# Tokens turned before their modulation is known, and three accumulator banks for the convolution stretch

## The reference, cut to what matters

```python
shift, scale, gate = split(silu(c) @ mod_w[li] + mod_b[li], 3)       # the same for c_ctx
hx = rms_norm(x, norm_w[li]) * (1.0 + scale) + shift
hc = rms_norm(ctx, norm_w[li]) * (1.0 + scale_c) + shift_c
```

## Time and profile before

| | |
|---|---|
| median of 3 runs | 1190.12 us (1187.65 to 1192.85) |
| the profiled execution's own time | 1189.36 us |
| its span in the trace | 1187.4 us |
| PE busy | 1113.2 us, 94% |
| DVE busy | 590.1 us, 50% |
| ACT busy | 359.4 us, 30% |
| POOL busy | 182.0 us, 15% |
| mean granted PE clock | 0.984 |
| DMA | 94.16 MB, mean 79 GB/s |

### The profile page before, as it was taken

One profiled execution on the slowest core, in us unless ns is written; L12 is line 12 of the kernel. 1 busy time (PEld: TensorE's weight loads), 2 busy tenths in 40 slices (PEclk: granted clock), 3 DMA queues, 4 the chain that ended last, 5 costly groups with the idle time before them and its releaser, 6 DMA issues.

```text
span 1187.4 us, 11863 instructions
## 1 busy us (share of the span) xinstructions
PE 1113.2 (94%) x4259; PEld 595.1 (50%) x4259; DVE 590.1 (50%) x1219; ACT 359.4 (30%) x822; POOL 182.0 (15%) x174
## 2 busy tenths in 40 slices
PE   3797889999998999999999999999999999999988
PEld 0474455545554444555544444444545555556654
DVE  0335356737683746676621114530346563446776
ACT  1522021214442234455410112111324433343450
POOL 2200100027772310000000001320012120000000
PEclk9899899999998999999999999999999999999999
DMA  9722404136667011001001104220110220200001
GB/s 309 286 71 75 141 1 142 68 123 202 201 219 247 34 54 39 16 1 54 1 1 56 68 0 155 71 71 24 48 66 6 72 106 1 72 1 1 1 1 71
DMA packets 47201, 94.16 MB, mean 79 GB/s; under 512 B 2870, under 2 KB 4567, under 8 KB 47143
## 3 DMA queue, kind: packets, MB, share of 16 engines
q1 hardware_dynamic: 42693, 81.41, 19.8%
q10 hardware_dynamic: 3330, 8.67, 2.0%
q0 software_dynamic: 1120, 3.32, 1.0%
HBM read 91.17 MB, written 2.23 MB: 79 GB/s over the span
## 4 chain that ended last, share of the span: by engine, by line
PE 87%; DVE 6%; DMA 4%; issue 1%; ACT 1%; SPq 1%; POOL 0%; DVEq 0%; ACTq 0%
PE ps L715 47%; PE ps L965 10%; PE ps L893 7%; PE ps L1001 4%; PE ps L1023 3%; PE ps L865 2%; DVE pool_mem L1154 2%; PE ps L912 2%; PE ps L877 2%; PE ps L944 2%; PE ps L1013 2%; PE ps L934 2%; DMA ring<-in_mod_w_dram 2%; PE ps L732 2%; PE ps L754 1%
## 5 line engine op out<-in xcount | busy, mean ns | idle before, releaser
L715 PE MATMUL ps<-ring,hT 128*128 128x512 f32 (+1 forms) x832 | 345.6, 573 | 2.2 <-DVE hT L1138 2.2
L715 PEld LDWEIGHTS ps<-ring,hT 128*128 128x128 f32 x832 | 156.7, 191 | 172.6 <-issue 165.0
L715 PE MATMUL ps<-hT,ring 128*128 128x512 f32 (+1 forms) x512 | 174.9, 500 | 15.5 <-DVE pool_mem L1154 15.5
L715 PEld LDWEIGHTS ps<-hT,ring 128*128 128x128 f32 x512 | 99.6, 197 | 85.4 <-issue 77.8
L1767 POOL TENSOR_SCALAR stat<-stat 128x8 f32<-128x8 f32 (+3 forms) x52 | 22.8, 439 | 717.6 <-DVE stat L1326 238.4
L893 PE MATMUL ps<-ring,hT 128*128 128x512 f32 x192 | 88.9, 594 | 0.8 <-DVE pool_mem L1381 0.8
L965 PE MATMUL ps<-ring,hT 128*128 128x512 f32 x192 | 85.7, 593 | 2.1 <-DMA ring<-in_ev_w_out_dram 2.1
L1358 DVE TENSOR_REDUCE stat<-ps 128x1 f32<-128x768 f32 x64 | 60.9, 952 | 52.4 <-PE ps L1001 52.2
L1425 DVE TENSOR_TENSOR pool_mem<-ps,pool_mem 128x512 f32<-128x512 f32 x36 | 24.8, 688 | 92.7 <-PE ps L965 87.5
L1768 POOL TENSOR_TENSOR stat<-stat 128x8 f32<-128x8 f32 (+3 forms) x52 | 66.4, 1278 | 4.3
L1154 DVE SCALAR_TENSOR_TENSOR pool_mem<-ps,halftap,pool_mem 128x254 f32<-128x254 f32 (+3 forms) x96 | 59.1, 616 | 3.4
(11 more groups left out here) (198 smaller groups left out, 1392.4 us busy)
## 6 DMA issues: line engine op xcount, KB each, us to landing
ring<-in_mod_w_dram SPq DMA_DIRECT2D x11, 2048.0 KB, 8.0
ring<-in_od_w_in_dram SPq DMA_DIRECT2D x8, 2048.0 KB, 8.3
ring<-in_ev_w_in_dram SPq DMA_DIRECT2D x7, 2048.0 KB, 8.2
pool_mem<-la_rows_dram SPq DMA_DIRECT2D x24, 512.0 KB, 7.0
ring<-in_ev_w_out_dram SPq DMA_DIRECT2D x4, 1536.0 KB, 6.6
ring<-in_od_w_out_dram SPq DMA_DIRECT2D x2, 2048.0 KB, 7.7
ring<-in_mod_w_dram ACTq DMA_DIRECT2D x1, 2048.0 KB, 14.3
xs_all<-in_x_dram POOLq DMA_DIRECT2D x4, 512.0 KB, 8.9
```

The source lines that it names most:

```text
L715: mm = pe.matmul(bank[:, 0:width], lhs_of(k), rhs_of(k), start=(k == 0), stop=(k == count - 1))
```

## The change

Beginning: the six token tiles are loaded first, from ACT's queue. SP loads only the identity, `pick` and the first parameter rows, then `mod` 0 to 3 and `kvdt` at once (`mod` 3 and `kvdt` have places of their own in memory that is free then), then the second parameter rows and the other constants. POOL's eight broadcast loads come after the last `norm`. A new stage `trt` turns a normalised tile, and DVE (first four feature blocks) and ACT (last four) copy it to `hT` as it is; a new stage `hmod` scales and shifts `hT` in place, a third of the tokens at a time, each third before two `kvdt` tiles. `params` 1 moves behind `kvdt` 1, three small DVE operations into `dtv`.

Convolution stretch: from `kvdt` 0 to the last `diag`, units take the least recently used of banks 0, 1 and 7, and `diag` is a unit.

Scan: fillers are `mod` in steps 1, 3, 5, 7 and 9 and `ga` in steps 2, 4, 6, 8, 10 and 11; step 0 has none.

The diff, cut to its core:

```diff
@@ stages_layer0
-    st = [("params", 0), ("params", 1)]
-    st += [("mod", 0, 0), ("mod", 0, 1), ("modsum", 0, 0), ("mod", 0, 2), ("modsum", 0, 1)]
-    st += [("norm", 0, t) for t in range(NT)]
-    st += [("mod", 0, 3), ("modsum", 0, 2), ("modsum", 0, 3), ("modcol", 0)]
-    st += [("trn", 0, k, 0) for k in range(KD)] + [("trn", 0, k, 1) for k in range(0, KD, 2)]
+    st = [("params", 0), ("norm", 0, 0), ("norm", 0, 1), ("trt", 0), ("norm", 0, 2), ("trt", 1), ("mod", 0, 0)]
+    st += [("norm", 0, 3), ("trt", 2), ("norm", 0, 4), ("trt", 3), ("mod", 0, 1), ("modsum", 0, 0)]
+    st += [("norm", 0, 5), ("trt", 4), ("trt", 5), ("mod", 0, 2), ("modsum", 0, 1), ("mod", 0, 3)]
+    st += [("modsum", 0, 2), ("modsum", 0, 3), ("modcol", 0)] + [("hmod", n) for n in range(3)]
+    for t in range(NT):
+        st += [("kvdt", t)] + ([("params", 1)] if t == 1 else [])
...
-    fill = [("ga", f, s) for f in range(1, 4) for s in range(2)]
-    mods = [(1, s) for s in range(1, 6)]
+    fill = {1: ("mod", 1, 1), 2: ("ga", 1, 1), 3: ("mod", 1, 2), 4: ("ga", 2, 1), 5: ("mod", 1, 3), 6: ("ga", 1, 0),
+            7: ("mod", 1, 4), 8: ("ga", 2, 0), 9: ("mod", 1, 5), 10: ("ga", 3, 0), 11: ("ga", 3, 1)}
@@ units
+BANKS = (0, 1, 7)
+THREE_BANKS = range(UNIT[("kvdt", 0)], max(UNIT[s] for s in UNITS if s[0] == "diag") + 1)
+for _n in range(len(UNITS)):
+    _b = min(range(3 if _n in THREE_BANKS else 2), key=lambda b: _last[b])
+    UNIT_BANK.append(_b)
...
@@ build
+        mod_slab = carve(512, KD * SLAB).rearrange("p (k n) -> p k n", k=KD)
+        kv_slab = carve(4608, KD * KVDT).rearrange("p (k n) -> p k n", k=KD)
@@ sync
-            for n in range(1, RING):
-                load_slab(n)
+            for part in range(4):
+                load_slab(SLAB_NO[("mod", 0, part)])
+            load_slab(SLAB_NO[("kvdt",)])
...
@@ tensor
+                elif kind == "trt":
+                    t = a[0]
+                    pe.wait_ge(xhat_ready, t + 1)
+                    for b in range(2):
+                        if t >= 2:
+                            pe.wait_ge(xt_done[b], t - 1)
+                        for j in range(4):
+                            k = 4 * b + j
+                            mm = pe.transpose(ps[:, 2 + 2 * (t % 2) + b, j * P:(j + 1) * P],
+                                              xhat[:, t, k * P:(k + 1) * P], ident)
+                        mm.then_inc(xt_ready, 1)
@@ vector (scalar is the same for k in range(4, KD), with ACT.Identity)
+                elif kind == "hmod":
+                    n = a[0]
+                    col = 8 * (n == 2)
+                    dve.wait_ge(cols_ready, 1)
+                    dve.wait_ge(xt_done[0], 2 * n + 2)
+                    for k in range(4):
+                        part = hT[:, k, 2 * n * P:2 * (n + 1) * P]
+                        last = V.tensor_scalar(part, part, gain_cols[:, col + k:col + k + 1],
+                                               mod_cols[:, 2 * col + k:2 * col + k + 1], ALU.mult, ALU.add)
+                    last.then_inc(h_done[0], 1)
@@ scalar
-            act.dma_start(slab_ap(SLABS[0]), slab_source(SLABS[0])).then_inc(slab_in[0], 16)
+            for t in range(NT):
+                src = x_in[t * P:(t + 1) * P, :] if t < NX else ctx_in[(t - NX) * P:(t - NX + 1) * P, :]
+                act.dma_start(xin[:, t, :], src).then_inc(x_in_s[t], 16)
```

More of the change, by code:

```diff
@@ L87 @@
 T_ORDER = (4, 5, 0, 1, 2, 3)
+EXTRA_PLACES = {("mod", 0, 3): RING, ("kvdt",): RING + 1}
 def stages_layer0():
-    st = [("params", 0), ("params", 1)]
-    st += [("mod", 0, 0), ("mod", 0, 1), ("modsum", 0, 0), ("mod", 0, 2), ("modsum", 0, 1)]
-    st += [("norm", 0, t) for t in range(NT)]
-    st += [("mod", 0, 3), ("modsum", 0, 2), ("modsum", 0, 3), ("modcol", 0)]
-    st += [("trn", 0, k, 0) for k in range(KD)] + [("trn", 0, k, 1) for k in range(0, KD, 2)]
+    st = [("params", 0), ("norm", 0, 0), ("norm", 0, 1), ("trt", 0), ("norm", 0, 2), ("trt", 1), ("mod", 0, 0)]
[4 more added lines that the diff above has]
+        st += [("kvdt", t)] + ([("params", 1)] if t == 1 else [])
     conv_order = [8, 9, 10, 11, 0, 1, 2, 3, 4, 5, 6, 7]
-    st += [("kvdt", t) for t in range(NT)] + [("dtv",)]
+    st += [("dtv",)]
     early = {3: (0, 4), 6: (0, 5), 10: (1, 0)}
@@ L141, in stages_layer0 @@
         last = None
[L142 to L147, removed]
+        if i in fill:
+            st.append(fill[i])
+            last, gated = (fill[i][1:], None) if fill[i][0] == "mod" else (None, fill[i][1:])
         if 1 <= i < len(STEPS) - 1:
@@ L280, in at @@
     return AT[stage]
-UNIT_STAGES = ("params", "mod", "modsum", "modcol", "xbc", "kvdt", "dt", "q", "ga", "z", "ytr", "out0",
+UNIT_STAGES = ("params", "mod", "modsum", "modcol", "xbc", "kvdt", "dt", "diag", "q", "ga", "z", "ytr", "out0",
                "k1", "v1", "q1", "g1", "hq", "hk", "pv1", "otr", "out1a", "out1b", "out1")
@@ L337 @@
 TRN = ordinal(("trn",))
-TRNS = len(TRN) // 2
+TRNS = len(TRN)
 STATEU = {}
@@ L581, in wait_done @@
             n = UNIT[stage]
-            eng.wait_ge(unit_done[n % 2], n // 2 + 1)
+            eng.wait_ge(unit_done[UNIT_BANK[n]], UNIT_TURN[n] + 1)
         def wait_done_upto(eng, stage):
             n = UNIT[stage]
-            for m in (n - 1, n):
-                eng.wait_ge(unit_done[m % 2], m // 2 + 1)
+            for m in range(n - (2 if n in THREE_BANKS else 1), n + 1):
+                eng.wait_ge(unit_done[UNIT_BANK[m]], UNIT_TURN[m] + 1)
         def bank_of(stage):
-            return ps[:, UNIT[stage] % 2, :]
+            return ps[:, BANKS[UNIT_BANK[UNIT[stage]]], :]
         def done_sem(stage):
-            return unit_done[UNIT[stage] % 2]
+            return unit_done[UNIT_BANK[UNIT[stage]]]
         def pair(n):
@@ L607, in slab_ap @@
             n = SLAB_NO[key]
+            if key in EXTRA_PLACES:
+                return mod_slab if key[0] == "mod" else kv_slab
             k = 6 if key[0] == "out0" else KD
@@ L1522, in _ @@
                                  ).then_inc(sq_ready, 1)
+                elif kind == "trt":
+                    t = a[0]
+                    act.wait_ge(xt_ready, 2 * t + 2)
+                    A.copy(hT[:, 4:KD, t * P:(t + 1) * P],
+                           ps[:, 3 + 2 * (t % 2), :].rearrange("p (k t) -> p k t", k=4)).then_inc(xt_done[1], 1)
+                elif kind == "hmod":
+                    n = a[0]
+                    col = 8 * (n == 2)
+                    act.wait_ge(cols_ready, 1)
+                    act.wait_ge(xt_done[1], 2 * n + 2)
+                    for k in range(4, KD):
+                        part = hT[:, k, 2 * n * P:2 * (n + 1) * P]
+                        last = A.activation(part, part, ACT.Identity, scale=gain_cols[:, col + k:col + k + 1],
+                                            bias=mod_cols[:, 2 * col + k:2 * col + k + 1])
+                    last.then_inc(h_done[1], 1)
                 elif kind == "trn":
```

121 lines of the change are left out of this document (71 added, 50 removed).

## The result

The changed kernel takes 1157.24 us (median of 4 runs, 1156.45 to 1157.88) beside 1191.48 for the kernel before (4 runs, 1187.65 to 1192.98): ratio 0.9717, 95% interval 0.9691 to 0.9743. The prediction was 1162, within 1150 to 1176.

A forecast was written before the change was run, and what follows sets the result against it. The prediction took PE to bound the kernel, 87% of the chain that ended last. Gains of 4.6 + 11.4 + 5.0 + 6.5 = 27.5 us took 1189.4 to 1161.9, about 1162 us as median, range 1150 to 1176.

The forecast's parts named there:

- The four terms of the sum: Gains of beginning 4.6, third bank 11.4, clock in the convolution 5.0 and scan 6.5 us, together 27.5 us.
- Beginning: Up to `kvdt`: starts at 46.5 instead of 52.97 us, less 1.9 for half clock; net gain 4.6 us, bounds -0.5 and 11.
- The charge for `kvdt`: At the start of `kvdt`: one start at half clock, 1.9 us, bounds nothing and 3.5.
- Banks: Convolution stretch: with three banks 7.9 of 19.3 us of PE's waits remain, at five places; 11.4 us gained.
- Clock in the convolution: Convolution stretch: half clock after waits costs 6.9 us before, 1.9 remain; 5.0 us gained.
- a rule of the Trainium skill: Convolution: every burst after a wait starts cold, so each of five remaining waits would be followed by a slow stretch.
- Scan: Scan: the stall at its end goes, 7.5 us, less slower short steps; net gain 6.5 us, bounds 1 and 8.
- a wait in step 5: Scan: POOL falls behind about half a microsecond a step, and step 5 waits about 1 us for `emul`.
- The first (the clock does not come back): Convolution: each of the five remaining waits costs 1.9 us of half clock; total 1170; chance 0.12.
- the second (the `kvdt` slab): Beginning: `kvdt`'s slab lands only at 53 us, so the beginning gains nothing; total 1168; chance 0.09.
- the third: Scan steps 1 to 5: POOL sets the pace, 9.1 us a step instead of 8.55; total 1168; chance 0.07.
- the fourth: Scan's short steps: `la_rows` blocks land too late, at 14 us or more; slower, total 1209; chance 0.06.

The follow-up runs named there:

- e1: The changed kernel with two banks again in the convolution stretch and `diag` back in bank 7, no unit: 1174.77 us.
- e3: The changed kernel with two banks again and the scan's fillers as before, so only the new beginning is left: 1181.43 us.
- e2: The changed kernel with the scan's fillers in their old order, everything else as changed: 1163.44 us.
- e4: The kernel before with `diag` made a unit and the rotation over banks 0, 1 and 7, old beginning and old fillers: 1168.90 us.
- e7: The changed kernel with all six `norm` and `trt` stages ahead of the first `mod`: 1158.01 us.
- e6: The changed kernel with 20 turns of 128x128 into bank 6, which nobody reads, before the first `kvdt`: 1158.31 us.

## Why the prediction was right

The four terms of the sum came out as large as forecast or larger: 27.5 us forecast, 32.6 in the spans, the 5.1 between them being 2.9 in the beginning, 1.5 in the clock of the convolution and 0.8 in the scan.

**Beginning: right, 3.5 us too careful.** The order and the releaser are those of the text: slab 0 at 16.75 (forecast 17), `hmod` last. The step that was mis-sized is the product at half clock: I charged the first at 3.64, and it took 1.99. With the second at full clock too (1.85), the scaling of tile 5 ended at 29.4 instead of 33, and the fourth product at 36.74 instead of 40.4. From there to the first use of the columns it was 40.88 - 36.74 = 4.1 (forecast 4.4 with a little overlap); the first `hmod` third took 2.05 us on ACT, from 40.88 to 42.93 (forecast 1.9). The charge for `kvdt` was 1.9, the trace shows 2.4. Net 7.5 us in the traces, against 4.6. A part of it is luck: 43.02 is the earliest start of six traces of this beginning, and in e1, where the first product did take 3.64, it is 44.98. The medians of e3 and e2 give 9.2 and 5.5 for the beginning. In the traces the stretch up to the end of `kvdt` is 5.9 us shorter (e3 beside before) and 8.7 (e2 beside e4); in the convolution behind it e3 is 2.4 shorter at the same waits, by clock, and e2 is 2.5 longer, 1.7 of them half clock.

**Banks: right to 0.1 us in the waits.** 7.9 us in five places, of 19.3. e4, with the old beginning, has the same waits less one of 0.98.

**Clock in the convolution: about right in size, wrong in which wait.** I expected half clock after 2.11 and none after 1.89; it was the other way round. 1.7 us remain, 1.9 forecast, and that they agree is luck: the same five waits left none in e4 (which has four of them), one in e2 and e7, and two in e6. Before, it had cost a little more than my 6.9: behind the `mod` of 3.64 the next 32 matmuls also took 11.36, against 10.59 behind one of 1.93 in e3. Gaps give 11.4 of the 17.9 us gained, and PE's busy time, 164.2 before and 157.7 after, the other 6.5, where I had 5.0.

The five waits of 0.98 to 2.11 us are followed by a slow burst once in the changed kernel. I had held a rule of the Trainium skill against them that does not speak of them: TensorE: Matmul & The Clock Gate, "HAM oscillation — how this bites in real kernels", has waits for DMA of some 3 to 5 us between its bursts, and there every burst starts cold. Of the waits of over 3 us here, in all traces, nine of twelve are followed by a slow burst: mostly as the page has it, but not always. The same page says under "What's actually happening" that the chip judges activity in windows that run freely and are not reset when a kernel starts; that would fit waits equal to 0.01 us with different ends, but no run here shows such windows.

**Scan: right, 0.8 too careful.** 5.75 us up to the last `intra`, and 1.5 behind it, where 32 matmuls take 13.95 instead of 15.56. I had charged 1 us for a wait in step 5 because POOL would fall behind. POOL is busy all 9.00 of 9.00 us, as foreseen, but the trace has one wait of 0.17 us in all short steps. e2 and e1 give 6.2 and 6.7 us for the fillers: POOL at its limit delayed nobody.

**The rivals.** The first (the clock does not come back) is refuted by the rows after five waits; the second (the `kvdt` slab) by a chain with no DMA after 16.75 us; the third and the fourth by 0.2 us of `emul` waits, the fourth also by the `la_rows` blocks, which landed 4.7 to 9.2 us after their issue and not at 14.

## What to carry to other kernels

List the units in the order in which PE takes them, and write beside each accumulator bank who reads it out and how long that takes. PE waits when it comes back to a long read-out too soon, and what a third bank saves came out of such a list to 0.1 us. The list has to run to the place where the rotation ends, as my two misses, 2.08 and 4.58 us, both lay in its last units, and it has to hold what the reading engine does before the read-out: 2.8 of the 4.58 us and the last 1.13 were DVE's backlog. The part that moves work ahead of a late operand is priced best by what each engine must do in order, not by the bytes. A clock charge after a wait is to be taken as an average over several traces: count how many waits of a length are followed by it, not which.

## What the runs showed of the hardware that was not expected

- Half clock after a wait isn't set by the wait's length alone. 3.81 and 3.18 us were followed by it in e1 and not in e3; 3.04 was in both, and not in the kernel before; 1.89 was after the change, and not before. Over all 14 traces, of the waits in the convolution none of 15 of 0.98 or 0.99 us is followed by it, 3 of 13 of 1.89 to 1.96, and 19 of 25 of 2.08 to 4.58.
- PE starts `kvdt` at half clock behind single turns, sums and a wait of 2.6 us, and the first 32 matmuls then take 9.7 to 10.5 us in seven traces. With 20 turns filling that wait they take 8.00, in all five kernels that have them.
- POOL with no idle time in a short step (9.00 of 9.00 us) cost the step nothing.
- In-place scaling of 128x256 within SBUF is quicker on DVE than from the accumulator, 0.41 us on average beside 0.54, and no quicker on ACT, 0.59 beside 0.56. In a row they overlap a little: twelve take 4.0 us of DVE and 6.0 of ACT.
